# Expert down-projection weights loaded two adjacent rows per partition, and the gated activations turned with a column step of two

## What is computed

```python
def ec_moe(h, router_w, w_gate, w_up, w_down):
    ...
    gate, idx = lax.top_k(jnp.swapaxes(aff, 1, 2), cap)
    flat = idx.reshape(B, N_EXPERTS * cap)
    xg = jnp.take_along_axis(h, flat[..., None], axis=1).reshape(B, N_EXPERTS, cap, D)
    a = jax.nn.silu(jnp.einsum('becd,edf->becf', xg, w_gate)) * jnp.einsum('becd,edf->becf', xg, w_up)
    y = jnp.einsum('becf,efd->becd', a, w_down) * gate[..., None].astype(h.dtype)
    return jnp.zeros_like(h).at[jnp.arange(B)[:, None], flat].add(y.reshape(B, N_EXPERTS * cap, D))
```

## Time and profile before

| what | value |
|---|---|
| median of 3 runs | 1557.84 us (1555.29 to 1558.34) |
| the profiled execution | 1554.0 us |
| its span, first to last instruction | 1552.2 us |
| PE, DVE, ACT, POOL busy in the span | 88%, 66%, 45%, 16% |
| weights of the experts | 192 loads of 1024 KB |
| mean granted clock of TensorE | 0.916 of full speed |

### The profile page before, as it was taken

The page is one execution under the profiler, slowest core; times in us unless marked ns, Lnnn a source line. Parts: engine busy times, 40 slices in busy tenths (PEclk is TensorE's granted clock), DMA queues, the critical chain, the costliest instruction groups (busy, mean ns, idle before and its releaser), DMA issues.

```text
span 1552.2 us, 18203 instructions
## 1 busy us (share of the span) xinstructions
PE 1361.0 (88%) x6827; PEld 1012.6 (65%) x6827; DVE 1017.9 (66%) x1091; ACT 704.6 (45%) x674; POOL 254.3 (16%) x161
## 2 busy tenths in 40 slices
PE   6888988899698989785998986899999999999993
PEld 1577877788687879662787743566666666666662
DVE  1765134452776868672325465899889999889992
ACT  2322234443343535322212104666667667666761
POOL 1021001110000000000000000124431324444411
PEclk9899989899699999858989877999999999999997
DMA  9403201113103121316006337899999999999993
GB/s 363 139 26 130 83 9 45 49 36 113 58 1 99 46 89 53 105 59 240 27 1 232 122 137 281 295 361 354 381 368 371 376 357 377 366 359 374 374 354 85
DMA packets 111666, 298.67 MB, mean 192 GB/s; under 512 B 6853, under 2 KB 32837, under 8 KB 111561
## 3 DMA queue, kind: packets, MB, share of 16 engines
q1 hardware_dynamic: 108344, 286.87, 50.9%
q0 software_dynamic: 3264, 11.01, 3.1%
HBM read 281.09 MB, written 19.40 MB: 194 GB/s over the span
## 4 chain that ended last, share of the span: by engine, by line
PE 68%; DVE 16%; issue 6%; ACT 6%; DMA 2%; POOL 1%; DVEq 0%; SPq 0%; ACTq 0%; POOLq 0%
PE ps L1528 17%; PE ps L1529 17%; PE ps L1530 17%; PE ps L1594 4%; PE ps L1698 4%; DVE w_lo L1458 3%; ACT w_hi L1011 2%; DVE w_lo L1056 1%; ACT w_hi L832 1%; PE ps L1649 1%; ACT arena L836 1%; DVE arena L1474 1%; DMA arena<-in_w_mod_dram 1%; DMA arena<-in_w_out_dram 1%; PE ps L1773 1%
## 5 line engine op out<-in xcount | busy, mean ns | idle before, releaser
L1458 DVE TENSOR_TENSOR w_lo<-arena,w_hi 128x2048 fp32r<-128x2048 f32 x192 | 435.4, 2287 | 63.3 <-ACT w_hi L1011 51.6
L1528 PE MATMUL ps<-w_hi,act_hi 128*80 128x512 f32 (+1 forms) x1048 | 419.1, 400 | 36.5 <-DVE w_lo L1458 22.8
L1529 PE MATMUL ps<-w_lo,act_hi 128*80 128x512 f32 (+1 forms) x1048 | 414.3, 395 | 0.0
L1530 PE MATMUL ps<-w_hi,act_lo 128*80 128x512 f32 (+1 forms) x1048 | 413.1, 394 | 0.0
L1011 ACT ACTIVATE w_hi<-arena 128x2048 fp32r<-128x2048 f32 x180 | 343.2, 1915 | 143.6 <-PE ps L1530 143.6
L1528 PEld LDWEIGHTS ps<-w_hi,act_hi 128*80 128x80 f32 (+1 forms) x1048 | 168.6, 161 | 122.7 <-DVE w_lo L1458 29.5
L1530 PEld LDWEIGHTS ps<-w_hi,act_lo 128*80 128x80 f32 (+1 forms) x1048 | 168.4, 161 | 75.5 <-issue 1.2
L1529 PEld LDWEIGHTS ps<-w_lo,act_hi 128*80 128x80 f32 (+1 forms) x1048 | 168.9, 161 | 69.0 <-issue 1.1
L1528 PE MATMUL ps<-act_hi,w_hi 128*128 128x320 f32 x576 | 189.6, 329 | 5.3 <-DVE act_lo L1363 5.3
L1529 PE MATMUL ps<-act_lo,w_hi 128*128 128x320 f32 x576 | 183.5, 319 | 0.0
L1530 PE MATMUL ps<-act_hi,w_lo 128*128 128x320 f32 x576 | 183.1, 318 | 0.0
(11 more groups left out here) (189 smaller groups left out, 1344.5 us busy)
## 6 DMA issues: line engine op xcount, KB each, us to landing
arena<-in_w_exp_gate_dram SPq DMA_DIRECT2D x64, 1024.0 KB, 8.8
arena<-in_w_exp_up_dram SPq DMA_DIRECT2D x64, 1024.0 KB, 7.2
arena<-in_w_exp_down_dram SPq DMA_DIRECT2D x64, 1024.0 KB, 6.8
arena<-in_w_mod_dram SPq DMA_DIRECT2D x24, 1024.0 KB, 6.4
arena<-in_w_in_dram SPq DMA_DIRECT2D x18, 1024.0 KB, 5.4
arena<-in_w_in_dram SPq DMA_DIRECT2D x12, 512.0 KB, 4.5
gl_raw<-arena SPq DMA_DIRECT2D x32, 160.0 KB, 1.8
arena<-gl_raw SPq DMA_DIRECT2D x8, 640.0 KB, 8.0
```

The source lines that it names most:

```text
L1458: v.tensor_tensor(Wl[sl], eraw[slot], Wh[sl].bitcast(F32), ALU.subtract).then_inc(s_el, 1)
L1528: t.matmul(out, sh, mh, start=start, stop=False)
L1529: t.matmul(out, sh, ml, start=False, stop=False)
L1530: return t.matmul(out, sl, mh, start=False, stop=stop)
```

## The change

The loads of down-projection pieces use another split of the 256 rows over the partitions: partition p now takes the adjacent rows 256k+2p and 256k+2p+1. These are 8 KB in one run, in memory and in the buffer, where there were two runs of 4 KB. In the built program the source pattern of a down load is `[2048, 128], [1, 2048]` instead of `[1024, 128], [131072, 2], [1, 1024]`, and that of the buffer has one run of 2048 too. Gate and up loads stay as they are. The 1 MB that a load fetches is the same 1 MB.

So block 2k of the contraction is now the even rows of the piece and block 2k+1 the odd ones, and `turn_a` reads the columns of `aa` to match: block q starts at column 256(q//2) + q%2 and takes every second column. In the built program the stationary operand of these transposes has the pattern `[2, 128]` where it had `[1, 128]`; count, sizes, order and outputs are the same. No instruction of any engine moves, and no wait is added or dropped.

```diff
@@ -701,7 +701,8 @@
             wg, wu, wd = (A[n][0] for n in ("w_exp_gate", "w_exp_up", "w_exp_down"))
 
             def epiece(w, e, k, slot):
-                src = w[bass.ds(e, 1), bass.ts(k, 2 * P), :].rearrange("a (k p) n -> p (a k) n", p=P)
+                order = "a (p k) n -> p (a k) n" if w is wd else "a (k p) n -> p (a k) n"
+                src = w[bass.ds(e, 1), bass.ts(k, 2 * P), :].rearrange(order, p=P)
                 sp.dma_start(eraw[slot].rearrange("p (k n) -> p k n", k=2), src).then_inc(s_er[slot], 16)
 
 
@@ -1808,7 +1809,8 @@
             def turn_a(e):
                 pe.wait_ge(s_a, e + 1)
                 for q in range(KD):
-                    ins = t.transpose(pair(3)[:, P * q:P * q + CAP], aa[0:CAP, P * q:P * q + P], ident[0:CAP, 0:CAP])
+                    c0 = 2 * P * (q // 2) + q % 2
+                    ins = t.transpose(pair(3)[:, P * q:P * q + CAP], aa[0:CAP, c0:c0 + 2 * P - 1:2], ident[0:CAP, 0:CAP])
                 ins.then_inc(s_aT, 1)
 
             def body(e, first=False, last=False):
```

## The result

| | before | changed |
|---|---|---|
| median | 1555.29 us (1551.63 to 1558.34, 19 runs) | 1560.25 us (1558.15 to 1564.25, 19 runs) |
| ratio to before | | 1.0033, 95% interval 1.0025 to 1.0041 |
| the profiled execution's span | 1552.2 us | 1560.9 us |

The change costs 5.0 us, 0.33%. The time lies in the predicted range, but "no change" at 76% was the wrong case: this is rival 1, at a smaller size than its middle amount of 11.2 us.

The account below looks back on a forecast made before the run. It took PE, with one stretch of ACT and DVE, to pace the expert loop while DMA follows. Loads 0, contention 0 and transposes 0 left the median at 1557.8 us, range 1552.5 to 1567.

Parts of the forecast that it names:

- no change: Whole kernel: loads, contention and transposes each add 0, so the median stays at 1557.8 us; chance 76%.
- rival 1: Expert loop, turn_a on PE: strided stationary loads are slower and lengthen the path, 11.2 to 16.8 us; chance 11%.
- middle amount: turn_a: the step between stationary loads doubles, 0.093 us more for each of 120 transposes, 11.2 us, giving 1569.
- What bounds the kernel: Expert loop: PE with one stretch of ACT and DVE sets the pace, 35.83 us per expert; full DMA engines only follow.
- Part one, the loads: Down-projection loads: 8 KB runs remove 8,192 packets, but nobody waits for these loads, so gain and cost are 0.
- The room: Down loads: a piece lies ready 5.9 us before ACT reads it, so somewhat faster or slower landings change nothing.
- Part two, where it lies: turn_a, in the PE-only stretch: any growth lengthens the expert, for 15 of 16 experts; the first is hidden.
- Part two, the price: turn_a's strided stationary loads: bounded between 0 and 16.8 us, taken as 0 because elements seemed to be read singly.
- the end's: turn_a, upper bound: the whole 140 ns load is added to each of 120 transposes without overlap, 16.8 us, giving 1574.6.
- Rivals 2, 3, 4: Down loads: larger runs make loads waited for, 3%; easier loads save time, 9%; runs stay 4 KB packets, 15% within no change.
- small amounts of rival 1: turn_a: strided transposes cost only 3 to 8 us, given some of the 11% weight and included in the range.

## Why the prediction was wrong, by its steps

- **What bounds the kernel**: right. PE paces, the loads follow. The down loads, a third of all, went in half as many packets, and no wait for a load came or went, in the changed kernel and in the run of the loads alone.
- **Part one, the loads, 0**: right in the loop. The room was 5.9 us, the landing went from 6.8 to 6.6 us and the issue from 373 to 336 ns, and none of it was on the path.
- **Part two, where it lies**: right. turn_a is uncovered, 15 of 16 count, 120 transposes. That the first is hidden stands too: PE starts again 7.45 us after turn_x with and without the step. A side effect by the clock in that stretch stays open, as said above.
- **Part two, the price: the step that failed.** "I take 0, as the 0.7 ns per column is nearest to a reader that takes single elements." The transposes cost 0.35 us an expert, 15 times. The 0.7 ns came from (0.79 - 0.14) / 7 = 0.093 us, and that was misread from the earlier trace rows: the first load of the eight had started 0.23 us ahead of the second, and this head start was averaged in. The other seven followed each other at 0.070 us, as the matmuls did (0.56 / 8), 0.55 ns a column; I had the 0.07 in rival 1 and took the loads to be slower. Columns read with a step took 0.453 us / 512 = 0.88 ns each in the run with the streamed operand, and 0.91 / 8 / 128 = 0.89 ns in turn_a. With neighbours the stream runs at 0.230 / 512 = 0.45 ns, twice that pace. So neighbours are read faster than columns with a step, and the premise under the 0 was false. How the reader does it, no run shows. A hint was in the trace before: on the streamed operand, neighbours were read at 0.45 ns a column in every 128x512 matmul.
- **The page I leaned on.** The Trainium skill, page "SBUF — State Buffer", section "Door 1: The DMA port swizzle", says that two hits on a line of 16 bytes are enough for full rate. Here the measurement differs: two hits a line (step of two) cost as much as one (step of four), 216 and 218 ns against 140, so the measurement decides. The 11% for rival 1 were too few, since this sentence and the premise above were the only things against it.
- **Rival 1's size**: per transpose 0.35 / 8 = 0.044 us against the middle's 0.093 and the end's 0.140. 120 x 0.044 = 5.3 us; measured 5.0.
- **Rivals 2, 3, 4**: all out. No wait for a load, no time given back, packets fell by 8,193 against 8,192 forecast (8,192 in the run of the loads alone).
- **The level**: I carried the median of 3 runs, 1557.84; over 19 it is 1555.29. The predicted 1557.8 for "no change" and the 1560.25 measured lie only 2.4 us apart, and not 5.0, for that reason. That nearness is luck: the level was 2.5 us too high, and the missed cost was 5.0. The place inside the range is not owed to it, since the range took in the small amounts of rival 1.

## What to carry to other kernels

When DMA engines look full, first ask whether anyone waits for a transfer; if not, a better access pattern for the loads buys nothing, as here, and what it asks of another engine is its whole price. Put a reordering where it is free: on ACT and DVE reading PSUM it cost nothing here; on TensorE's stationary operand a load took half as much again, and on its streamed operand a matmul took twice the time. And a short block on the engine that paces belongs in front of that engine's own wait, not behind it: moving eight transposes by one piece gave more than the whole change cost.

## What the hardware showed that I had not expected

- A stationary fp32 operand of 128 columns read with a step loads in 216 ns in place of 140, and eight such transposes take 0.91 in place of 0.56 us. Steps of two, three and four cost alike (216, 214, 218 ns), a step of eight a little less (205).
- The loads of back-to-back transposes follow each other at 0.070 us with neighbours and at 0.116 with a step of two; the first starts 0.23 us ahead, so the mean spacing over all eight misleads.
- A streamed operand read with a step of two (in a pattern of three dimensions) takes 0.453 us for 512 columns in place of 0.230, at the full clock.
- ACT and DVE read PSUM with a step of two at the pace of neighbours: 1000 and 1209 ns for 80x1024, against 1004 and 1210.
- An 8 KB run is one packet, SP issues such a load in 336 ns in place of 373, and the landing does not change by more than two profiles of the same loads differ (6.6 us against 6.8).
